# The last rows of a decoder step: sums of squares made with channels on partitions, and norm weights folded into the turning matmuls

## What is computed

```python
def _rms_norm(x, g):
    x32 = x.astype(jnp.float32)
    y = x32 * lax.rsqrt(jnp.mean(x32 * x32, axis=-1, keepdims=True) + RMS_EPS)
    return (y * g.astype(jnp.float32)).astype(x.dtype)
...
    x = x + (jax.nn.silu(gate) * up) @ w_down[l]
y = _rms_norm(x, norm_final)
```

## Time and profile before

| | |
|---|---|
| median of 3 runs | 1762.29 us (1762.21 to 1763.51) |
| profiled execution | 1762.81 us |
| its span | 1761.0 us |
| mean granted TensorE clock | 0.997 |
| PE (matmuls) busy | 1740.2 us, 99% |
| VectorE (DVE) busy | 838.3 us, 48% |
| ScalarE (ACT) busy | 517.9 us, 29% |
| GpSimd (POOL) busy | 948.7 us, 54% |
| chain that ended last | PE 93%, DVE 3%, DMA 1%, ACT 1% |

### The profile page before, as it was taken

One profiled execution on the slowest core, in us unless ns is written; L12 is line 12 of the kernel. 1 busy time (PEld: TensorE's weight loads), 2 busy tenths in 40 slices (PEclk: granted clock), 3 DMA queues, 4 the chain that ended last, 5 costly groups with the idle time before them and its releaser, 6 DMA issues.

```text
span 1761.0 us, 29821 instructions
## 1 busy us (share of the span) xinstructions
PE 1740.2 (99%) x12458; PEld 1704.2 (97%) x12458; DVE 838.3 (48%) x928; ACT 517.9 (29%) x942; POOL 948.7 (54%) x520
## 2 busy tenths in 40 slices
PE   7999999999999999999999999999999999999998
PEld 7999999999999999999989999999999999999998
DVE  5733322455555154546837787444544444533213
ACT  6533321012010244556102234333333333101003
POOL 3788873323323422223437449987888886355550
PEclk9999999999999999999999999999999999999999
DMA  7333324123133525265724431222222223723212
GB/s 247 120 121 99 122 94 156 34 78 112 52 96 99 174 64 168 89 211 166 194 84 133 144 132 51 93 97 72 78 89 72 72 72 105 267 69 125 63 56 97
DMA packets 165118, 196.51 MB, mean 112 GB/s; under 512 B 7305, under 2 KB 139649, under 8 KB 165033
## 3 DMA queue, kind: packets, MB, share of 16 engines
q1 hardware_dynamic: 137168, 152.72, 26.8%
q10 hardware_dynamic: 27865, 42.56, 7.2%
HBM read 137.27 MB, written 57.99 MB: 111 GB/s over the span
## 4 chain that ended last, share of the span: by engine, by line
PE 93%; DVE 3%; DMA 1%; ACT 1%; issue 0%; SPq 0%; POOL 0%; DVEq 0%; POOLq 0%; ACTq 0%
PE unit_ps L1050 42%; PE pair_ps L1112 36%; PE unit_ps L1498 4%; PE task_banks L1332 2%; PE task_banks L1305 1%; PE task_banks L1318 1%; PE task_banks L1229 1%; PE task_banks L1213 1%; PE task_banks L1206 1%; PE task_banks L1215 1%; DMA x_row<-in_x_prompt 1%; DVE s_lo L2177 0%; PE task_banks L1201 0%; PE task_banks L1186 0%; PE task_banks L1237 0%
## 5 line engine op out<-in xcount | busy, mean ns | idle before, releaser
L1050 PE MATMUL unit_ps<-a_hi,w_part 128*128 128x344 f32 x2592 | 523.3, 327 | 2.0 <-ACT a_hi L1573 1.6
L912 POOL TENSOR_TENSOR w_part<-w_raw,consts 128x1024 fp32r<-128x1024 f32 (+1 forms) x69 | 164.4, 2383 | 588.7 <-PE unit_ps L1050 530.7
L1050 PEld LDWEIGHTS unit_ps<-a_hi,w_part 128*128 128x128 f32 x2592 | 422.1, 188 | 10.9 <-issue 8.0
L1050 PE MATMUL unit_ps<-a_lo,w_part 128*128 128x344 f32 x1296 | 275.3, 321 | 0.7 <-DVE a_lo L2163 0.7
L1112 PE MATMUL pair_ps<-a_hi,slots_a 128*128 128x258 f32 x1536 | 258.1, 283 | 1.6 <-DVE a_lo L2177 1.3
L1050 PEld LDWEIGHTS unit_ps<-a_lo,w_part 128*128 128x128 f32 x1296 | 218.8, 189 | 1.0 <-DVE a_lo L2163 1.0
L1112 PEld LDWEIGHTS pair_ps<-a_hi,slots_a 128*128 128x128 f32 x1536 | 216.1, 190 | 2.1 <-DVE a_lo L2177 1.5
L915 POOL TENSOR_TENSOR w_part<-w_raw,w_part 128x1024 fp32r<-128x1024 f32 (+1 forms) x71 | 193.6, 2726 | 15.0 <-DVE a_lo L2163 9.7
L1602 ACT ACTIVATE snap<-pair_ps 128x516 f32<-128x516 f32 x128 | 77.0, 601 | 216.7 <-PE pair_ps L1112 216.7
L1112 PE MATMUL pair_ps<-a_lo,slots_b 128*128 128x258 f32 x768 | 139.7, 284 | 0.0
L2186 DVE TENSOR_TENSOR h_out<-pair_ps,snap 128x516 f32<-128x516 f32 x64 | 44.4, 694 | 198.7 <-ACT snap L1602 128.4
(11 more groups left out here) (290 smaller groups left out, 3013.3 us busy)
## 6 DMA issues: line engine op xcount, KB each, us to landing
w_raw<-in_w_in SPq DMA_DIRECT2D x38, 512.0 KB, 3.9
h_spill<-h_out SPq DMA_DIRECT2D x11, 1032.0 KB, 5.0
raw_a<-in_w_gate_up SPq DMA_DIRECT2D x11, 1024.0 KB, 6.8
raw_b<-in_w_gate_up SPq DMA_DIRECT2D x11, 1024.0 KB, 5.1
gate_spill<-stage ACTq DMA_DIRECT2D x16, 516.0 KB, 2.8
a_lo<-h_spill SPq DMA_DIRECT2D x15, 516.0 KB, 5.3
w_raw<-in_w_down SPq DMA_DIRECT2D x16, 448.0 KB, 3.6
att_in<-att_spill ACTq DMA_DIRECT2D x3, 2048.0 KB, 7.9
```

The costliest lines, as they stand in the source:

```text
L912: pool.tensor_tensor(part[:, 0], raw, one, ALU.mult).then_inc(w_high, 1)
L1050: mm = pe.matmul(unit_ps[s][:, n, 0:PIECE], w_part[:, slot, w, k0 + by * k, :], x[:, k, n * PIECE:(n + 1) * PIECE], start=(k == 0 and part ...
```

## The change

It touches only the tail.

1. `diag_gain` (128 x 8 x 128, in the space of `temp`) is made by VectorE: for each channel block, the identity times the norm's weights.
2. Tiles 5, 6 and 7 are turned not by a transpose but by a plain matmul with `diag_gain` as the moving operand, so that they come out times the weights (`turn_rest`). Their first seven channel blocks are turned between units 6 and 7 of `U_REST`; the last block after unit 7 has been added. The sample rows are turned in the same way, into the third banks of the unit tiles, after the roots have been taken.
3. For rows 640 to 1031 the sums of squares are made with channels on partitions: ScalarE squares each block of `wide` after its addition (128x392), VectorE adds blocks 1 to 6 to the sum, and TensorE sums over partitions with a column of ones (eight one-column matmuls, the last square added by accumulation).
4. ScalarE takes two roots, VectorE two reciprocals (`factor_of`). ScalarE scales tiles 5 and 7 out of PSUM, VectorE tile 6 and the sample rows (from two banks).
5. SP waits for the engine that makes each tile; the sample rows are stored from `y_square`.

Cut to its core (declarations of semaphores are left out):

```diff
+        tail_space = temp[:].rearrange("p a b -> p (a b)")
+        diag_gain = tail_space[:, 0:D].rearrange("p (k c) -> p k c", k=KT)
+        rest_sum = tail_space[:, D:D + REST]
+        rest_sq = tail_space[:, D + REST:D + 2 * REST]
+        rest_rows = slice(EARLY_TILES * P, TOKENS)
+        rest_ps = unit_ps[0][:, 2, REST_SUMS:REST_SUMS + 4]
+        root_of, factor_of = gains[:, 1, 0:4], gains[:, 1, 4:8]
+        sample_ps = (unit_ps[1][0:SAMPLES, 2, :], unit_ps[0][0:SAMPLES, 2, :])
...
+                if t < EARLY_TILES:
+                    sp.wait_ge(y_ready, t + 1)
+                elif t == EARLY_TILES + 1:
+                    sp.wait_ge(y_ready, EARLY_TILES + 1)
                 else:
-                    sp.dma_start(out["y_sample"][:, 0, :], y_row[0:SAMPLES, t % 3, :]).then_inc(y_stored[t % 3], 16)
+                    sp.wait_ge(y_scaled, 1 + (t - EARLY_TILES) // 2)
+                sp.dma_start(out["y_prompt"][0, t * P:(t + 1) * P, :], y_row[:, t % 3, :]).then_inc(y_stored[t % 3], 16)
+            sp.wait_ge(y_ready, EARLY_TILES + 2)
+            sp.dma_start(out["y_sample"][:, 0, :], y_square[0:SAMPLES, :]).then_inc(y_stored[CHUNKS % 3], 16)
...
+            def turn_rest(t, k):
+
+                return pe.matmul(y_ps[t % 3][:, k // 4, (k % 4) * P:(k % 4 + 1) * P], wide[:, k, t * P:(t + 1) * P],
+                                 diag_gain[:, k, :], start=True, stop=True)
...
-            for g in range(2):
-                pe.wait_ge(unit_free[g], U_FINAL // 2)
-            for t in range(EARLY_TILES, CHUNKS + 1):
-                turn_rows(t)
+                if m == KT - 2:
+                    pe.wait_ge(diag_ready, 2)
+                    pe.wait_ge(unit_free[1], Place(U_REST).half(m - 1) + 1)
+                    for t in range(EARLY_TILES, CHUNKS):
+                        pe.wait_ge(y_ready, t - 2)
+                        for k in range(m):
+                            turn_rest(t, k)
+                    pe.wait_ge(unit_free[0], Place(U_REST).half(m) + 1)
+                    for t in range(EARLY_TILES, CHUNKS):
+                        turn_rest(t, m)
+
+            pe.wait_ge(unit_free[1], U_FINAL // 2)
+            for t in range(EARLY_TILES, CHUNKS):
+                turn_rest(t, KT - 1).then_inc(y_turned, 1)
+            pe.wait_ge(rest_acc, KT - 2)
+            pe.wait_ge(rest_square, KT)
+            for i in range(4):
+                n = P if i < 3 else SAMPLES
+                c = slice(i * P, i * P + n)
+                pe.matmul(rest_ps[0:n, i:i + 1], rest_sum[:, c], const("ones")[:, 0:1], start=True, stop=False)
+                mm = pe.matmul(rest_ps[0:n, i:i + 1], rest_sq[:, c], const("ones")[:, 0:1], start=False, stop=True)
+            mm.then_inc(rest_total, 1)
+            pe.wait_ge(rest_root, 2)
+            for k in range(KT):
+                mm = pe.matmul(sample_ps[k // 4][:, (k % 4) * P:(k % 4 + 1) * P], wide[:, k, SEQ:TOKENS], diag_gain[:, k, :],
+                               start=True, stop=True)
+            mm.then_inc(y_turned, 1)
...
+            for m in range(KT):
+                act.wait_ge(unit_free[m % 2], Place(U_REST).half(m) + 1)
+                act.activation(rest_sq if m else rest_sum, wide[:, m, rest_rows], ACT.Square).then_inc(rest_square, 1)
+                if m < EARLY_TILES:
+                    tile_square(m)
+
+            act.wait_ge(rest_total, 1)
+            for n, c in ((P, slice(0, 3)), (SAMPLES, slice(3, 4))):
+                act.activation(root_of[0:n, c], rest_ps[0:n, c], ACT.Sqrt, scale=1.0 / D, bias=const("eps", n)[:, 0:1])\
+                   .then_inc(rest_root, 1)
+            act.wait_ge(rest_factor, 2)
+            for i in (0, 2):
+                t = EARLY_TILES + i
+                act.wait_ge(y_turned, t + 1)
+                act.wait_ge(y_stored[t % 3], 16 * (t // 3))
+                act.activation(y_row[:, t % 3, :].rearrange("p (a b) -> p a b", a=2), y_ps[t % 3], ACT.Copy,
+                               scale=factor_of[:, i:i + 1]).then_inc(y_scaled, 1)
...
             dve.wait_ge(gain_loaded, 16)
+            dve.tensor_tensor(diag_gain, const("ident").unsqueeze(1).to_broadcast([P, KT, P]),
+                              gain_row[:].rearrange("p (k c) -> p k c", k=KT), ALU.mult).then_inc(diag_ready, 1)
             for m in range(KT):
                 take(Place(U_REST), m)
                 x = wide[:, m, EARLY:TOKENS]
                 dve.tensor_tensor(x, unit_ps[m % 2][:, 2, 0:TOKENS - EARLY], x, ALU.add).then_inc(unit_free[m % 2], 1)
+                if 1 <= m < KT - 1:
+                    dve.wait_ge(rest_square, m + 1)
+                    wait(dve, rest_acc, m - 1)
+                    dve.tensor_tensor(rest_sum, rest_sum, rest_sq, ALU.add).then_inc(rest_acc, 1)
                 if 1 <= m <= EARLY_TILES:
                     y_out(m - 1)
-            for t in range(EARLY_TILES, CHUNKS + 1):
-                y_out(t)
+
+            dve.wait_ge(rest_root, 2)
+            dve.reciprocal(factor_of[:, 0:3], root_of[:, 0:3]).then_inc(rest_factor, 1)
+            dve.reciprocal(factor_of[0:SAMPLES, 3:4], root_of[0:SAMPLES, 3:4]).then_inc(rest_factor, 1)
+            t = EARLY_TILES + 1
+            dve.wait_ge(rest_factor, 2)
+            dve.wait_ge(y_turned, t + 1)
+            dve.wait_ge(y_stored[t % 3], 16 * (t // 3))
+            dve.tensor_scalar(y_row[:, t % 3, :].rearrange("p (a b) -> p a b", a=2), y_ps[t % 3],
+                              factor_of[:, 1:2], None, ALU.mult).then_inc(y_ready, 1)
+            dve.wait_ge(y_turned, CHUNKS + 1)
+            for x in range(2):
+                ins = dve.tensor_scalar(y_square[0:SAMPLES, x * 4 * P:(x + 1) * 4 * P], sample_ps[x],
+                                        factor_of[0:SAMPLES, 3:4], None, ALU.mult)
+            ins.then_inc(y_ready, 1)
```

More of the change, by code:

```diff
@@ L81 @@
 EARLY_TILES = EARLY // P
+REST = TOKENS - EARLY_TILES * P
+REST_SUMS = 400
 HALF, QUAD, KH = TOKENS // 2, TOKENS // 4, KT // 2
@@ L536, in build @@
         y_ready = sem("y_ready")
+        y_scaled = sem("y_scaled")
+        rest_square = sem("rest_square")
+        rest_acc = sem("rest_acc")
+        rest_total = sem("rest_total")
+        rest_root = sem("rest_root")
+        rest_factor = sem("rest_factor")
         y_stored = [sem(f"y_stored{i}") for i in range(3)]
@@ L881, in _ @@
             sp.dma_start(gain_row[:], a["norm_final"].partition_broadcast(P)).then_inc(gain_loaded, 16)
[L882 to L886, removed]
-                else:
-                    sp.dma_start(out["y_sample"][:, 0, :], y_row[0:SAMPLES, t % 3, :]).then_inc(y_stored[t % 3], 16)
+            for t in range(CHUNKS):
+                if t < EARLY_TILES:
+                    sp.wait_ge(y_ready, t + 1)
+                elif t == EARLY_TILES + 1:
+                    sp.wait_ge(y_ready, EARLY_TILES + 1)
+                else:
+                    sp.wait_ge(y_scaled, 1 + (t - EARLY_TILES) // 2)
+                sp.dma_start(out["y_prompt"][0, t * P:(t + 1) * P, :], y_row[:, t % 3, :]).then_inc(y_stored[t % 3], 16)
+            sp.wait_ge(y_ready, EARLY_TILES + 2)
+            sp.dma_start(out["y_sample"][:, 0, :], y_square[0:SAMPLES, :]).then_inc(y_stored[CHUNKS % 3], 16)
             for g in range(3):
@@ L2101, in _, with tile_square @@
                     row_part(c, k)
-            for t in range(CHUNKS + 1):
-                n, g = P if t < CHUNKS else SAMPLES, t % 3
+            def tile_square(t):
+                g = t % 3
                 act.wait_ge(y_turned, t + 1)
[L2106 to L2110, removed]
+                wait(act, act_step, 2 * t)
+                act.activation(y_square[:].rearrange("p (a b) -> p a b", a=2), y_ps[g], ACT.Square,
+                               accum_out=fin[:, g, 0:1]).then_inc(act_step, 1)
                 act.wait_ge(act_step, 2 * t + 1)
-                act.activation(fin[0:n, g, 0:1], fin[0:n, g, 0:1], ACT.Sqrt, scale=1.0 / D, bias=const("eps", n)[:, 0:1])\
+                act.activation(fin[:, g, 0:1], fin[:, g, 0:1], ACT.Sqrt, scale=1.0 / D, bias=const("eps")[:, 0:1])\
                    .then_inc(act_step, 1)
+            for m in range(KT):
[14 more added lines that the diff above has]
+                               scale=factor_of[:, i:i + 1]).then_inc(y_scaled, 1)
         @block.vector
@@ L2814, in y_out @@
             def y_out(t):
-                n, g = P if t < CHUNKS else SAMPLES, t % 3
+                g = t % 3
                 dve.wait_ge(act_step, 2 * t + 2)
                 wait(dve, y_stored[g], 16 * (t // 3))
-                step(dve.reciprocal(fin[0:n, g, 1:2], fin[0:n, g, 0:1]))
+                step(dve.reciprocal(fin[:, g, 1:2], fin[:, g, 0:1]))
                 step.settle()
-                ps = y_ps[g][0:n]
-                dve.scalar_tensor_tensor(out=y_row[0:n, g, :].rearrange("p (a b) -> p a b", a=2), in0=ps,
-                                         scalar=fin[0:n, g, 1:2], in1=gain_row[0:n, :].rearrange("p (a b) -> p a b", a=2),
```

(4 more changed lines are left out.)

## The result

The changed kernel takes 1766.83 us (median of 12 runs, 1765.68 to 1770.48) against 1762.4 us before: ratio 1.0023, interval 1.0016 to 1.003. It is slower by 0.2%, and the forecast was 1766.4. Its profiled execution has a span of 1765.4 us.

What follows compares the result with a forecast made beforehand. PE, busy 99% of the span, was taken to bound the kernel until unit 7's end. 4.7 us ahead plus a tail of 10.4 instead of 11.0 gave +4.1 on 1762.29, so 1766.4 us; range 1764.2 to 1768.4.

Steps and rivals of the forecast that it cites:

- The turning ahead: Between units 6 and 7 on PE: 21 plain turning matmuls lengthen the path one for one, +4.7 us.
- What was costed at nothing: Ahead of unit 7: `diag_gain` (1.2 us), squares and additions (about 0.5 us each) hide in ScalarE's and VectorE's gaps.
- Behind A: After VectorE's addition of unit 7 ends: last turnings, sums, roots, scaling and stores take 10.4 us instead of 11.0.
- The drain: At the end: three 512 KB stores land back to back, 3 x 1.22 us, and become the last thing.
- one of the signs named: In the profile after, at the kernel's end: the chain of waits would end in DMA; no size given.
- The sum: Whole span: 4.7 us ahead plus a tail of 10.4 minus 11.0 gives +4.1 us.
- one record a matmul: Rival for the turning matmuls: each costs one record like a transpose, so +0.6 us, 1762.9 us; chance 0.09.
- table load: Rival behind VectorE's last addition: a ScalarE table load of 1.28 us lands on the chain, 1767.7 us; chance 0.06.
- The four-fold price: Rival for the turning matmuls: each costs four times a transpose, 0.44 us, so +11.0 us, 1773 us; chance 0.03.
- The last rival: Rival for the tail: it is not shortened at all, +4.7 to +6 us, 1767 to 1768.3 us; chance 0.03.

Runs made afterwards that it cites:

- e1: Changed kernel with tiles 5, 6 and 7 turned by transposes at the same places, leaving out the norm's weights there; 1764.73 us, ratio 1.001 to before.
- e3: Changed kernel with all 24 plain turning matmuls run behind VectorE's last addition, none ahead of unit 7; 1765.11 us, ratio 1.0011 to before.
- e7: Changed kernel without the sample rows' turning and scaling, and with the last three stores carrying 512 of 1024 columns; 1765.07 us, ratio 1.0013 to before.
- e6: Changed kernel without the turning and scaling of the eight sample rows, their store still issued; 1766.75 us, ratio 1.0018 to before.
- e5: The changed kernel run again with nothing altered; 1767.0 us, ratio 1.0023 to before.
- e2: Changed kernel with the stores of tiles 5, 6 and 7 carrying only 512 of 1024 columns; 1766.87 us, ratio 1.0021 to before.
- e4: Changed kernel with its eight one-column matmuls for the sums issued twice, same result; 1768.93 us, ratio 1.0036 to before.

## Why the prediction was right

- **The turning ahead** (4.7 us, path one for one): 4.69 measured, A moved by that much. e1 shows that it is the price per record, e3 that the place makes it a loss.
- **What was costed at nothing** held. The three units in a row and the transposes ahead take the times they took; VectorE's additions of squares (0.57 us each) and ScalarE's squares (0.53) fall into their gaps, and PE never waits for `y_ready`. The cover is thinnest at unit 6, where VectorE idles only 0.23 us before its addition.
- **Behind A** the terms came out a little shorter: the sums 1.6 us instead of 1.75 (16 records at 0.11 each were taken; the last four, with 8 columns of weights, took 0.24 together), roots and reciprocals 0.67 instead of 0.79, first scaled tile at A + 4.2 instead of 4.45, sample rows at 6.2 instead of 6.4, end at 10.2 instead of 10.4.
- **The drain** was named as the last thing: 3.85 us without a gap, one 0.82 after the first issue, as worked out. e7 against e6 shows it by taking half of the bytes. One of the signs named did not appear: the chain as the profile gives it does not end in DMA but with the sample rows' scaling (1760.02, then `DVEq`), so the drain has to be read from the stretches and from SP's last wait.
- The sum gave +4.1 on the span; 4.69 + 10.2 - 11.0 = +3.9 is what the tail did, and 99.0 - 95.1 from B to the end says the same (e5: +4.1). The medians differ by 4.4, the ratio says 0.16 to 0.3%.
- **What the prediction did not see** is the clock. It took the sample rows' turning at 1.8 us, and in four of the profiles (e1, e2, e4, e5) it took 3.3 to 3.6. It did little harm (10.4 in e5 against 10.2). At full clock the path through the sample rows would end at about A + 8.5 (ready at 6.2, and 2.3 from there to the end as in e2), 1.7 us ahead of the drain, and the slower clock took 1.4 to 1.7 of that. That it fitted was luck of the sizes, not part of the working.
- The rivals: one record a matmul fell with L1533's 42 records. No table load stands behind A (ScalarE's timeline above has none). The four-fold price of the Trainium skill (TensorE: Matmul & The Clock Gate, Terms) doesn't hold here: e1 and the changed kernel give 0.109 and 0.223 us for the same turning in a row of 21, a factor of two. The last rival, a tail that is not shortened, falls with 10.2 against 11.0.

## What to carry to other kernels

Where one engine is busy to the end, work moved ahead of its last step costs its full length; behind the last step the same work may run beside others. So first ask which part of it stood on the path (here 8 of 24 transposes, 0.9 of 2.6 us), and whether it stays at its old price when its form changes (a transpose by a plain f32 matmul doubled it).

When several results become ready together, their stores queue: the end is then the first store's issue plus the bytes of all, and a shorter computation helps only as far as the first store starts sooner. Two small gains were found in the tail: sums of squares made early, which need nothing of PE ahead of A (0.9 us), and two tiles left instead of three (0.8 us). Neither shows in a median by itself, and together they gave 1.7 us.

## What the hardware showed beyond that

- A one-column f32 matmul with 128x128 weights takes 0.111 us a record, as much as one with 128 columns; four with 128x8 weights took 0.24 together, from the first start to the last end.
- The granted clock fell from 2.4 to 1.2 GHz in the tail of some executions and not of others, with the same program: it stayed at 1.00 in the changed kernel's first profile until 1763.5, and was at 0.5 from 1757.0 in e5. Ahead of the fall PE had gone from the dense units to short and one-column matmuls, with the pause for VectorE's addition between them, but so it had in the first profile. The place differs: within the sums in e4 (1757.1), with their end in e5 and e2 (1757.0 and 1758.0), among the sample rows in e1 (1753.9). Matmuls of 128 columns then took about 0.21 us a record (3.35 / 16) instead of 0.12. What decides between the two wasn't settled.
- Single 512 KB stores landed 2.6 us after their issue. The Trainium skill (DMA: Bandwidth & Descriptors, Anatomy of one DMA — SWDGE (gpsimd) path) gives 2.0 us plus the bytes at 436 GB/s for DMAs on GpSimd's path, which would be 3.2 us, an estimate from it. These stores are issued by SP, on another path: the rate is close (410 to 426 GB/s while all 16 engines were busy), and the fixed part was 1.4 us here.
